# Four orderings in a two-block transformer kernel: decay scans between two rotations, decays behind an eviction, and norms' square sums and latent attention some steps later

## The reference, cut to what matters

```python
# first block: gated linear attention (GLA), 4 heads, 64 channels of q and k, 128 of v, two directions
q_g = axial_rope(heads(q_g, GLA_HEADS), row_pos, col_pos) * GLA_DK ** -0.5
k_g = axial_rope(heads(k_g, GLA_HEADS), row_pos, col_pos)
la_f, la_b = log_decay(z_lr, gla_w_alpha[layer], gla_b_alpha[layer])
o_g = gla_bidir(q_g, k_g, heads(v_g, GLA_HEADS), la_f, la_b, s_ctx_f, s_ctx_b)
#   in gla_chunked: b = jnp.cumsum(log_a...) within chunks of 64 tokens
#   q_dec = qc * exp(b);  k_inv = kc * exp(-b);  k_end = kc * exp(b_last - b);  decay = exp(b_last)
...
# second block, two layers: latent attention, convolution and retention branches
q = (rms_norm(c_q, q_norm) @ w_uq)             # latent norms: 256 and 128 channels
kv = (rms_norm(c_kv, kv_norm) @ w_ukv)
...
y = jax.nn.silu(layer_norm(y, ln_g, ln_b))      # conv norm, 512 channels, after 31 taps
...
on = ((of - mu) * lax.rsqrt(var + EPS))         # retention norm, 256 channels for each of 4 heads
```

## Time and profile before

| | us |
|---|---|
| median of 3 runs | 2887.31 (2887.26 to 2887.69) |
| the profiled execution | 2887.51 |
| its span, first to last instruction | 2885.5 |
| PE busy | 2813.1 |
| DVE busy | 1284.7 |
| ACT busy | 1136.1 |
| POOL busy | 1193.7 |
| mean granted PE clock | 0.996 |

### The profile page before, as it was taken

One profiled execution on the slowest core, in us unless ns is written; L12 is line 12 of the kernel. 1 busy time (PEld: TensorE's weight loads), 2 busy tenths in 40 slices (PEclk: granted clock), 3 DMA queues, 4 the chain that ended last, 5 costly groups with the idle time before them and its releaser, 6 DMA issues.

```text
span 2885.5 us, 34416 instructions
## 1 busy us (share of the span) xinstructions
PE 2813.1 (97%) x13718; PEld 2245.5 (78%) x13718; DVE 1284.7 (45%) x1706; ACT 1136.1 (39%) x1687; POOL 1193.7 (41%) x539
## 2 busy tenths in 40 slices
PE   7999999999999999999999999999999999999999
PEld 6778778888888776787788888867757868788887
DVE  4776424611113867735315202277677353341123
ACT  4334643432233555433334322245555233443222
POOL 2123234354443662453444444436625434344442
PEclk9999999999999999999999999999999999999999
DMA  7344223333333220222232323332202323333332
GB/s 257 117 145 136 78 81 109 105 111 101 95 95 126 81 66 30 73 95 74 88 124 81 102 92 98 96 108 76 66 30 81 95 66 104 98 106 95 95 95 80
DMA packets 89278, 277.97 MB, mean 96 GB/s; under 512 B 9952, under 2 KB 10272, under 8 KB 89120
## 3 DMA queue, kind: packets, MB, share of 16 engines
q1 hardware_dynamic: 89120, 275.78, 29.4%
HBM read 268.40 MB, written 7.34 MB: 96 GB/s over the span
## 4 chain that ended last, share of the span: by engine, by line
PE 89%; DVE 8%; ACT 2%; issue 1%; DMA 0%; SPq 0%; DVEq 0%; ACTq 0%
PE bank L1684 23%; PE bank L1686 23%; PE bank L1685 23%; PE bank L2010 2%; PE bank L1817 2%; PE bank L1960 1%; PE bank L1734 1%; PE bank L1733 1%; PE bank L1735 1%; PE bank L1710 1%; PE bank L1972 1%; PE bank L1702 1%; PE bank L1703 1%; PE bank L2001 1%; DVE pageF L2819 1%
## 5 line engine op out<-in xcount | busy, mean ns | idle before, releaser
L2957 POOL TENSOR_TENSOR wlo<-wraw,whi 128x1024 fp32r<-128x1024 f32 x429 | 1042.8, 2433 | 1479.9 <-ACT whi L2039 1465.3
L1684 PE MATMUL bank<-pageR,whi 128*128 128x512 f32 x3184 | 1286.0, 404 | 6.4 <-ACT pageF L2292 1.6
L1686 PE MATMUL bank<-pageR,wlo 128*128 128x512 f32 x3184 | 1230.8, 387 | 0.0
L1685 PE MATMUL bank<-pageR,whi 128*128 128x512 f32 x3184 | 1229.6, 386 | 0.0
L1684 PEld LDWEIGHTS bank<-pageR,whi 128*128 128x128 f32 x3184 | 599.6, 188 | 158.8 <-issue 40.1
L1685 PEld LDWEIGHTS bank<-pageR,whi 128*128 128x128 f32 x3184 | 599.9, 188 | 135.7 <-issue 22.8
L1686 PEld LDWEIGHTS bank<-pageR,wlo 128*128 128x128 f32 x3184 | 599.0, 188 | 123.8
L2039 ACT ACTIVATE whi<-wraw 128x1024 fp32r<-128x1024 f32 x429 | 450.9, 1054 | 411.9 <-PE bank L1686 320.2
L2113 ACT ACTIVATE pageR<-pageF 128x512 fp32r<-128x512 f32 x136 | 86.1, 633 | 423.8 <-DVE pageF L2678 188.7
L2819 DVE SCALAR_TENSOR_TENSOR pageF<-pageF,prm 128x497 f32<-128x497 f32 (+9 forms) x180 | 189.5, 1053 | 2.5
L2966 POOL TENSOR_TENSOR pageR<-pageF,pageR 128x512 fp32r<-128x512 f32 x46 | 66.2, 1447 | 141.2 <-ACT pageR L2113 105.6
(11 more groups left out here) (236 smaller groups left out, 2609.4 us busy)
## 6 DMA issues: line engine op xcount, KB each, us to landing
wraw<-in_wst SPq DMA_DIRECT2D x429, 512.0 KB, 3.5
pageF<-in_wmod SPq DMA_DIRECT2D x96, 256.0 KB, 4.7
pageF<-in_xT SPq DMA_DIRECT2D x16, 256.0 KB, 4.1
pageF<-in_bias SPq DMA_DIRECT2D x16, 256.0 KB, 3.9
kept<-pageF SPq DMA_DIRECT2D x16, 256.0 KB, 4.7
pageF<-kept SPq DMA_DIRECT2D x16, 256.0 KB, 4.0
out_x<-pageF SPq DMA_DIRECT2D x8, 256.0 KB, 2.0
pageF<-in_cT SPq DMA_DIRECT2D x4, 256.0 KB, 10.1
```

Source lines behind the costliest of these rows:

```text
L1684: e.matmul(o, hi, xh, start=first, stop=False)
L1685: e.matmul(o, hi, xl, start=False, stop=False)
L1686: i = e.matmul(o, lo, xh, start=False, stop=last)
L2957: e.tensor_tensor(wlo[:, b % NH, :, :], wraw[:, b % NR, :, :], bc(whi[:, b % NH, :, :]), ALU.subtract).then_inc(*wlod.up(("wlo", b)))
```

## The change

In `main_gla`, for the first pair, the main line yields once between the two rotations; the sides issue one step there, which is `gla_scan`. A name is added when the values of a head have been evicted, and `gla_backward` with all that follows it in `side_gla` waits for the name of the pair's second head. Between the two directions of the pair m, `side_gla` pauses 2*m yields. The latent norm's squares stand two yields ahead of their sum and not one, and four yields and not three stand between the latent norms and `make(0)`. The conv norm's squares stand four yields ahead of their sum and not two, the retention norm's three and not two. No computation is added or removed.

```diff
@@ main_gla
             if m:
                 evict(("kgc", m), ("oc", "wk_g", m), 256)
                 yield from proj("wq_g", m, H)
+            else:
+                yield
             rope_gla(("qg", m), ("o", "wq_g", m))
             for h in (2 * m, 2 * m + 1):
                 if h:
                     yield from proj("wv_g", h, H, HC)
                     evict(("vg_f", h), ("o", "wv_g", h))
                     evict(("vgc_f", h), ("oc", "wv_g", h), 256)
+                    made.add(("vg_f", h))
                 if h % 2:
                     gla_values(h - 1)
             yield
@@ side_gla
                 step("gla_scan", m, dr)
             yield
-            yield from p.ready(("kg", m), ("qg", m))
+            yield from p.ready(("kg", m), ("qg", m), ("vg_f", 2 * m + 1))
             step("gla_backward", m)
@@ side_gla
             for dr in range(2):
                 g = (m, dr)
-                yield from pause(0 if dr else 3)
+                yield from pause(2 * m if dr else 3)
                 to_tokens(("KT", g), ("KE", g), ALL4, sbk, ("ke", g))
@@ side_mla
-            yield
+            yield from pause(2)
             r = yield from s1.rstd_steps(128, "ones", sbk)
...
             pages.give(r, ("cqn", l, 1))
-            yield from pause(3)
+            yield from pause(4)
             live = set()
@@ side_ret
                     sq.add(("rof", l, h, i), 0, ("rof", l, h, i))
-                yield
-                yield
+                yield from pause(3)
                 r = yield from sq.rstd_steps(256, "ones", sbk)
```

## The result

The changed kernel takes **2899.7 us** (median of 5 runs, 2898.0 to 2900.6) against 2887.3 us: ratio 1.0042, 95% interval 1.0031 to 1.0053. It is **slower** by 12.4 us, where 17.1 us of gain were forecast. Lines of after and of the experiments stand one to five lower or higher than in before, by the lines that each edit adds; the text names them by their work.

The account below looks back on a forecast made before the run. The prediction took TensorE to bound the kernel, leaving only its 72 us of idle time or lowered clock to win. Terms 17.3 - 2.1 + 2.7 - 0.8 = 17.1 us gave 2870.2 us from 2887.31, range 2862 to 2881.

Parts of the forecast that it names:

- The ten norm waits: Layers: TensorE's ten waits for squares before norm sums (latent, conv, retention) all fit under added work; 12.0 us won.
- Conv: Conv norm in each layer: the 2.13 us wait goes and 1.7 us of lowered clock behind it.
- The layers' 17.3: Gain in both layers: 12.0 norm waits + 3.4 clock + 1.6 and 1.3 latent waits - 1.0 empty main steps.
- the clock's part: Behind the conv sum the clock of 0.74 over 6.6 us becomes full in both layers: 3.4 us won.
- Latent: Latent path, make(0) one step later: waits for mla_k's banks (1.6 us) and tanh_scaled (1.3 us) go.
- Retention: Retention norm, squares to sum 2 steps becomes 3: waits of 0.6 to 1.15 us, three heads a layer, go.
- First pair: First GLA pair: the 4.88 us eviction wait goes, the 0.90 us wait on qg's bank grows to some 5.5; gain 0.2.
- Second pair: Second GLA pair: gate 5.8 us later, mod_sum 1 at 167.6, gla_states waits for it; stage ends 2.1 us later.
- Attention, five steps later: First block's attention: the 2.68 us wait at 251.30 behind a softmax exponential goes; 2.7 us won, bounds 0 and 2.7.
- The end of the attention: First block: the last na_values fall behind the main line's end, leaving TensorE partly uncovered; 0.8 us lost, bounds 0 and 3.
- C: Rival: moved VectorE instructions meet GpSimd weight splits, some 1.3 us more each, about 7 us in all: 2877; chance 0.08.
- E: Rival: later attention, evictions get pages whose last reader was just planned, 2.7 us each; slower, some 2894; chance 0.05.

Follow-up runs that it names:

- attention_later: The kernel before the change with five empty steps ahead of the first block's attention, nothing else changed: 2886.0 us, ratio 1.0000.
- the four splits: The changed kernel with only four of 429 weight splits, those overlapping the two GLA-pair stalls, cut to 8 columns: 2888.0 us, 1.0006 of the unchanged kernel.
- conv_k: The kernel before the change with only the conv norm's pause (2 to 4 steps) and one step more before make(0): 2884.6 us, ratio 0.9995.
- k_ct: The kernel before the change with the conv and retention pauses and one step more before make(0): 2877.9 us, ratio 0.9970.
- conv_ret: The kernel before the change with only the conv norm's pause (2 to 4 steps) and the retention norm's (2 to 3): 2879.9 us, ratio 0.9977.
- latent_only: The kernel before the change with only the two latent edits (squares to sum 1 to 2 steps, make(0) one step later): 2892.7 us, ratio 1.0026.
- lat1_ct: The kernel before the change with the conv and retention pauses and the latent squares-to-sum step (1 to 2): 2880.6 us, ratio 0.9978.
- latent_2_small: The kernel with only the two latent edits, plus one GpSimd weight split a layer made small: 2886.9 us, 1.0003 of the unchanged kernel.
- norms_only: The kernel before the change with all four norm edits of the layers, first block left as it was: 2882.3 us, ratio 0.9985.
- conv_only: The kernel before the change with only the conv norm's pause (2 to 4 steps): ratio 0.9973, a gain of 7.8 us.

## Why the prediction was wrong, point by point

The forecast and the two profiled executions lie 30.0 us apart: 16.3 arose in the first block and 13.7 in the layers.

- **The ten norm waits: right.** 12.0 us gone, all ten. **Conv: right by itself**, 7.8 (4.6 to 10.7) against 7.7; that it agrees so closely is luck, since the 3.4 us of clock in it were read from one execution in which both layers had lost it. The layers' 17.3 became 3.6. Of the 13.7 missing, 8.5 are the latent path (2.9 gained in the forecast, 5.6 lost), 3.2 the halves of the retention, and 3.4 the clock's part, which didn't come: from the 3400th projection matmul on PE was busy for 1928.1 us, in before for 1928.0. Against them stands the 1.0 us for the empty steps, which wasn't paid.
- **Latent, "the waits for mla_k's banks (1.6 us) and for tanh_scaled (1.3 us) go": the first step that failed, in the layers.** They became one stall of 5.0 us a layer. I took the copies of mla_k for the only work ahead of tanh_scaled. Ahead of it stood the root, the norm and two taps, 3.7 us of them standing still beside one split and two halves. In numbers: where 2.9 us were to be gained, 5.6 were lost (10.0 against 1.6 + 1.3 and 1.5 for mla_q), and half clock with it.
- **Retention, its three waits a layer: they went, but what is late next was not named.** Each norm comes one step later, so do the halves on POOL, and PE waited 1.6 us a layer for them. In after the last half on POOL ran for 1.27 us from 1414.50 on, and the norm ahead of it on VectorE, at 1412.00, took 1.67 instead of 0.69.
- **First pair: the mechanism was right, its size was not.** One wait on the bank of the qg rotation, no other: 7.45 us against 5.5. The term "the scans took 80.14 to 84.97, 4.83 us" was read where no split ran; at the new place one of the eight instructions took 2.2 us more. In before the split of that time blocked only 0.4 us of a rotation (L2457 took 1.07).
- **Second pair: the place was right** (gla_states waits for mod_sum 1, at 168.64 against 167.6 forecast), the bank walk and the gate's shift with it. The second step that failed is the end of the stage, "From 167.6 on PE has 1.1 us less left", and with it the 2.1 us: I counted the stall as a shift of work and didn't ask what it does to the clock, which was 0.59 over 12 us, with the matmuls behind the stall at 1.2 GHz up to 176 us. The splits' cost was inside the 167.6, because the stretch of before has three encounters as well.
- **Attention, five steps later: the third step that failed, and by size the largest.** 2.7 gained was right for the wait of the earlier trace rows, which is gone, and wrong as "I take it, since the neighbouring steps of before show no such wait". Another took its place, 3.58 us, on the same ScalarE queue: an exponential behind a root, a table load of 1.28, a gate and a weight copy of 1.05 us; and 3.86, 1.16 and 0.74 us came elsewhere. The bound "nothing won" fits attention_later, where the shift stands alone. In after, 1.9 us of gain (2.7 - 0.8) became a part that is 10.8 us longer (a little of it GLA work that came over), far outside the bound. Of this the runs show the stalls and the half clock behind the two long ones, and that the four splits have no share in it. The 3.86 us go when all splits are small; by which way the splits make them is open. The end of the attention, 0.8, was right: 0.78.
- **The rivals.** C had the mechanism, but it priced an encounter at 1.3 us, and the runs have 1.9 to 2.2; and it counted encounters as additions to my sum, all on engines that had slack, and not what lies behind them: PE's stall, and its clock. It gave 2877 for what turned out as 2899.7. E alone had the side right, with another mechanism: none of the new waits read here ends at a page's last reader.

What is still open: why conv_k, k_ct and conv_ret differ as they do was read in traces, not tested; the load behind the 3.86 us likewise. What gives the first block its half clock behind the 3.58 us in after and not in attention_later is open too. Without the splits the change gains 1.4 us and not 17.1; what takes the rest there was not taken apart. And each trace is one execution: where the clock falls behind a short wait, it can be another place in the next.

## What to carry to other kernels

When work moves on an engine whose instructions another engine's can hold up, take its duration from the place where it will land, and look there for the other engine's long instructions: in this kernel one encounter costs 2 us, 4 of 429 splits decided over 10 us, and an edit that is right in its aim (all ten waits gone) lost more than it won. Before an eviction or a matmul is given more time, list everything that is queued ahead of whatever waits next, not only what is named in the edit; and test edits that aim at one stall each by themselves, since here one of seven (conv) gains 7.8 us by itself, and all seven together lose 12.4.

## What the runs showed of the hardware

- GpSimd's splits, busy for 1043 us, cost VectorE 201 us of standing still, although VectorE is busy for 45% only; the kernel is 27.5 us shorter with GpSimd almost silent.
- A stall of PE costs more than itself. Behind the stalls of 6.15 and 3.86 us the granted clock was 0.50 (1.2 GHz) from 168 to 176 and from 284 to 288 us; behind the 2.13 us of the conv sum it fell too, but only in six of the 18 places where profiled kernels have this wait.
- It can also cost nothing. In five kernels whose first block is that of before (latent_only, conv_ret, lat1_ct, conv_k, latent_2_small) the clock fell behind the 1.10 us wait at 138 us, in the other five (before, norms_only, k_ct, conv_only, attention_later) it did not; in the former the next fixed wait, for mod_sum 1, was 0.63 to 0.67 us instead of 2.28, and from the one wait to the end of the other it took 23.9 us in both kinds. So here half clock ahead of a wait on another engine was hidden by it.
